# A two-layer hybrid decoder on one core: the second half of the first layer's down projection with the activations stationary, seven of its 22 steps by seven block products, its result turned in the next layer

## The reference, cut to what matters

```python
h = rms_norm(x, ffn_norm_w[l])
ff = (jax.nn.silu(h @ w_gate[l]) * (h @ w_up[l])) @ w_down[l]   # w_down: 5632 x 2048
x = x + ff
# next layer
h = rms_norm(x, attn_norm_w[l + 1])
proj = h @ w_in[l + 1]
```

## Time and profile before

| | us |
|---|---|
| median of 3 runs | 2095.04 |
| the three runs | 2094.85 to 2095.5 |
| profiled execution, whole | 2095.22 |
| its span, first to last instruction | 2093.5 |
| TensorE busy in the span | 2085.8 |
| DVE busy / ACT busy / POOL busy | 1408.1 / 1037.2 / 216.8 |

### The profile page before, as it was taken

One profiled execution on the slowest core, in us unless ns is written; L12 is line 12 of the kernel. 1 busy time (PEld: TensorE's weight loads), 2 busy tenths in 40 slices (PEclk: granted clock), 3 DMA queues, 4 the chain that ended last, 5 costly groups with the idle time before them and its releaser, 6 DMA issues.

```text
span 2093.5 us, 37778 instructions
## 1 busy us (share of the span) xinstructions
PE 2085.8 (100%) x16266; PEld 1965.1 (94%) x16266; DVE 1408.1 (67%) x1635; ACT 1037.2 (50%) x1289; POOL 216.8 (10%) x289
## 2 busy tenths in 40 slices
PE   9999999999999999999999999999999999999999
PEld 8987899999999999889999878999999999998887
DVE  7887866555555556876578878664555555558888
ACT  5555754444444444544445557454444444445454
POOL 1034200001000010000000432000110001100000
PEclk9999999999999999999999999999999999999999
DMA  7675366677767777776656644666777776778785
GB/s 229 187 213 150 127 201 191 192 203 205 215 203 203 206 205 223 248 227 191 193 171 192 202 141 150 193 189 183 202 203 213 207 203 202 205 221 259 240 264 188
DMA packets 213591, 420.81 MB, mean 201 GB/s; under 512 B 13408, under 2 KB 13808, under 8 KB 213424
## 3 DMA queue, kind: packets, MB, share of 16 engines
q1 hardware_dynamic: 202752, 390.24, 61.9%
q0 software_dynamic: 10640, 28.15, 4.5%
q10 hardware_dynamic: 32, 0.01, 0.0%
HBM read 406.78 MB, written 11.57 MB: 200 GB/s over the span
## 4 chain that ended last, share of the span: by engine, by line
PE 98%; ACT 1%; DMA 0%; DVE 0%; issue 0%; SPq 0%; ACTq 0%; DVEq 0%
PE ps L871 67%; PE ps L626 11%; PE ps L649 10%; PE ps L666 2%; PE ps L665 2%; PE ps L664 2%; PE ps L708 1%; PE ps L850 1%; DMA raw<-in_w_in_dram 0%; PE ps L828 0%; PE ps L827 0%; PE ps L803 0%; PE ps L788 0%; ACT w_hi_s L1065 0%; PE ps L750 0%
## 5 line engine op out<-in xcount | busy, mean ns | idle before, releaser
L1354 DVE TENSOR_TENSOR w_lo_s<-raw,w_hi_s 128x1024 fp32r<-128x1024 f32 x504 | 624.9, 1241 | 528.0 <-ACT w_hi_s L1065 526.8
L871 PE MATMUL ps<-h_hi,w_hi_s 128*128 128x256 f32 x3192 | 883.7, 277 | 0.8 <-DVE xr L1446 0.8
L871 PE MATMUL ps<-h_hi,w_lo_s 128*128 128x256 f32 x3192 | 881.9, 276 | 0.0
L871 PE MATMUL ps<-h_lo,w_hi_s 128*128 128x256 f32 x3192 | 881.8, 276 | 0.0
L1065 ACT CAST w_hi_s<-raw 128x1024 fp32r<-128x1024 f32 x503 | 528.0, 1050 | 697.2 <-PE ps L871 675.4
L871 PEld LDWEIGHTS ps<-h_hi,w_hi_s 128*128 128x128 f32 x3192 | 599.4, 188 | 1.2 <-DVE xr L1446 1.0
L871 PEld LDWEIGHTS ps<-h_hi,w_lo_s 128*128 128x128 f32 x3192 | 599.5, 188 | 0.0
L871 PEld LDWEIGHTS ps<-h_lo,w_hi_s 128*128 128x128 f32 x3192 | 599.5, 188 | 0.0
L1065 ACT CAST w_hi<-raw 128x1024 fp32r<-128x1024 f32 x185 | 193.4, 1051 | 154.1 <-PE ps L649 64.2
L1354 DVE TENSOR_TENSOR w_lo<-raw,w_hi 128x1024 fp32r<-128x1024 f32 x185 | 230.1, 1256 | 44.0 <-ACT w_hi L1065 43.3
L871 PE MATMUL ps<-f_hi,w_hi_s 128*128 128x256 f32 x832 | 231.2, 278 | 0.4 <-DVE stage L1391 0.4
(11 more groups left out here) (272 smaller groups left out, 2260.7 us busy)
## 6 DMA issues: line engine op xcount, KB each, us to landing
...
```

The source lines that it names most:

```text
L871: done = nc.tensor.matmul(ps[:, bank + m // 2, m % 2 * TOK:(m % 2 + 1) * TOK], w[:, slot, k, m * P:(m + 1) * P], h[:, rows + k, :], start= ...
L1354: v_.tensor_tensor(lo[:, slot, :, :], raw[:, slot, :, :], hi[:, slot, :, :].bitcast(F32), ALU.subtract).then_inc(lo_split, 1)
```

## The change

Chunks 2 and 3 of layer 0 become a second run in the activations-stationary form (run 1; layer 1's runs are now 2 and 3), on the banks that layer 1's second run uses. Its steps 7, 9, ..., 19 are made by seven block products; steps 0 to 6 and the even ones are plain. The weights-stationary form and its buffers begin only with layer 1's pair 0, and `reaches_next` moves there. The result of the run is written to `t_raw` by `half_out(1, e)`, after the last two pairs of the layer. TensorE turns it in layer 1, chunk 2 after pair 0 and chunk 3 after pair 1. Chunks 0 and 1 are turned after step 1 of run 1. Layer 1's pair 0 now waits for `half_out(1, 0)`. In layer 1 DVE and ACT add, split and square chunks 2 and 3 in steps 0 to 6, and what hangs on the norm moves: `x_total` from after pair 5 to after pair 8, `dt_products` and `spread_rs` from 8 to 10, `channels` from 9 to 11, `conv` from 9-12 to 11-14, `silu` from 13 to 15. `conv_out` stays after pair 16. The running sums of squares move from `stage` to `vtok`.

```diff
     DOWN = FT // 2
-    STEPS = range(3, 20, 2)
+    STEPS = [range(3, 20, 2), range(7, 20, 2), range(3, 20, 2), range(3, 20, 2)]
...
 
     def weights_stationary(pair):
         layer, p = pair // PAIRS, pair % PAIRS
-        return p < 4 * PPG or P_OUT <= p < P_DOWN or p >= P_LATE and layer < DEPTH - 1
+        return p < 4 * PPG or P_OUT <= p < P_DOWN
...
+        if p < P_DOWN:
             return None
         half, rest = divmod(p - P_DOWN, 2 * DOWN)
-        return layer + half, rest // 2, rest % 2
+        return 2 * layer + half, rest // 2, rest % 2
 
     def seven(pair):
 
         step = down_step(pair)
-        return step is not None and step[1] in STEPS
+        return step is not None and step[1] in STEPS[step[0]]
 
     def seven_before(run, q):
 
-        return run * len(STEPS) + len([s for s in STEPS if s < q])
...
 
-        return 2 * ((layer * GROUPS_ALL + idx) % 2)
+        return 2 * (idx % 2)
 
     def in_bank(layer, g):
...
-        square_sums, chunk_sums = stage[:, 1, 0, 0:TOK], stage[:, 1, 0, TOK:2 * TOK]
+        kept_sums = vtok[:, :, :, :].rearrange("p t j d -> p (t j d)")
+        square_sums, chunk_sums = kept_sums[:, 0:TOK], kept_sums[:, TOK:2 * TOK]
 
         class Steps:
...
+            def turn_half(n):
+
+                pe.wait_ge(half_kept, n + 1)
+                turned(4 + 2 * (n % 2), chunk_tiles(lambda t: t_raw[:, t, n % 2, :]), half_turned)
...
                     elif layer:
-                        pe.wait_ge(down_added, layer * DCH - 1 + g)
+                        pe.wait_ge(half_kept, 4 * layer - 1 + g)
...
-                        if layer and p == 5:
+                        if layer and p in (0, 1):
+                            turn_half(2 + p)
+                        if layer and p == 8:
                             x_total(layer, 0)
...
-                        if p == 8:
+                        if p == (10 if layer else 8):
...
-                    if layer:
+                for run in range(2 * layer, 2 * layer + 2):
+                    if run == 2:
                         pe.wait_ge(back_ready, DCH)
-                    else:
+                    elif run == 0:
                         pe.wait_ge(vec_ready, layer + 2)
                     for q in range(DOWN):
-                        pair = base + P_DOWN + ((run - layer) * DOWN + q) * 2
-                        if run < DEPTH and q % 2 == 0:
+                        pair = base + P_DOWN + ((run - 2 * layer) * DOWN + q) * 2
+                        if run % 2 == 0 and q % 2 == 0:
                             pe.wait_ge(ff_lo, layer * FCH + (q // 2 + 1))
-                        if run < DEPTH and q == STEPS[0]:
+                        if run % 2 == 0 and q == STEPS[run][0]:
                             pe.wait_ge(gate_scaled, layer * FCH + FCH)
                             pe.wait_ge(ff_ready, layer * FCH + FCH)
-                        if run == DEPTH and q == 0:
+                        if run % 2 and q == 0:
                             pe.wait_ge(sums_added, run)
-                        if run == DEPTH and q == STEPS[0]:
+                        if run % 2 and q == STEPS[run][0]:
                             pe.wait_ge(down_added, layer * DCH + 2)
                         if seven(pair):
                             seven_products(pair, run, q)
...
-                    pe.wait_ge(sums_added, layer + 1)
-                    for q in range(DOWN):
-                        pair = base + P_DOWN + n * DOWN + q
-                        products_turned(pair % RING, pair, 2 * q, down_bank(layer, n), q == 0, q == DOWN - 1, f_hi, f_lo)
-                        if n == 2 and q == 4:
-                            for e in range(2):
-                                pe.wait_ge(half_kept, e + 1)
-                                turned(4 + 2 * e, chunk_tiles(lambda t: t_raw[:, t, e, :]), half_turned)
+                        if run == 1 and q == 1:
+                            for n in range(2):
+                                turn_half(n)
+
 
 
         @block.scalar
...
-                reaches_next = P_OUT <= p < P_OUT + RING - 1 or weights_stationary(pair) and P_LATE <= p < P_LATE + RING - 1
+                reaches_next = P_OUT <= p < P_OUT + RING - 1 or pair >= PAIRS and p < RING - 1
                 act.wait_ge(pair_used, pair + (2 if reaches_next else 1))
                 if not seven(pair) or down_step(pair)[2] == 0:
...
                         x_square((0, 1, 4, 5).index(p))
-                    if layer and p == 1:
-                        x_hi(layer, 0, 3)
-                        x_chunk_squares(layer, 0, 3)
-                    if p == 8:
+                    if layer and p in (2, 4):
+                        act.wait_ge(half_turned, 4)
+                        x_hi(layer, 0, 1 + p // 2)
+                    if layer and p in (3, 5):
+                        x_chunk_squares(layer, 0, p // 2 + 1)
+                    if p == (10 if layer else 8):
                         rsb_out(layer, 0)
                     if p % 8 == 7 and 32 < p < 63:
                         evacuate(layer, p // 8)
...
                         nc.scalar.activation(dte[:, :], togo[:, :], ACT.Exp).then_inc(ecum_ready, 1)
-                    if 13 <= p < 38 and p % 8 == 5:
+                    if p == (15 if layer else 13) or 21 <= p < 38 and p % 8 == 5:
...
                         keep_first(down_step(base + p)[0])
-                    if layer + 1 < DEPTH and p >= P_LATE:
-                        n, q = (p - P_DOWN) // DOWN, (p - P_DOWN) % DOWN
-                        if n == 2 and q in (8, 12):
-                            x_hi(layer + 1, 0, q // 4 - 2)
-                        if n == 2 and q in (9, 13):
-                            x_chunk_squares(layer + 1, 0, q // 4 - 2)
-                        if n == 3 and q == 1:
-                            x_hi(layer + 1, 0, 2)
-                        if n == 3 and q == 2:
-                            x_chunk_squares(layer + 1, 0, 2)
+                    if down_step(base + p) in ((1, 4, 0), (1, 5, 0)):
+                        n = down_step(base + p)[1] - 4
+                        act.wait_ge(down_added, n + 1)
+                        x_chunk_squares(layer + 1, 0, n)
+                    if down_step(base + p) in ((1, DOWN - 2, 1), (1, DOWN - 1, 0)):
+                        x_hi(layer + 1, 0, down_step(base + p)[1] - DOWN + 2)
 
 
...
 
-            def half_out(e):
-
-                dve.wait_ge(pair_used, P_LATE - 1 + e + RING)
+            def half_out(run, e):
+
+                dve.wait_ge(pair_used, P_DOWN + 2 * (run + 1) * DOWN - 1 + e + RING)
                 for t in range(T):
                     added = stage[:, (0, 1, 0, 1)[2 * t + e], (0, 0, 1, 1)[2 * t + e], :]
-                    last = v_.tensor_tensor(t_raw[:, t, e, :], ps[:, four_banks(0)[t][e], :], added, ALU.add)
+                    last = v_.tensor_tensor(t_raw[:, t, e, :], ps[:, four_banks(run)[t][e], :], added, ALU.add)
...
 
-                if n < 2:
-                    dve.wait_ge(half_turned, n + 1)
-                else:
-                    dve.wait_ge(pair_used, layer * PAIRS + (P_DOWN + (n + 1) * DOWN + RING))
+                dve.wait_ge(half_turned, n + 1)
                 v = xr[:, :, n * N:(n + 1) * N]
...
                         split_lo(ahead_pair)
-                    if layer and p == 1:
-                        x_lo(layer, 0, 3)
-                    if layer and p == 3:
-                        sum_squares(layer, 0, 3)
-                    if p == 6:
+                    if layer and p in (0, 2, 4):
+                        x_lo(layer, 0, 1 + p // 2)
+                    if layer and p in (1, 3):
+                        add_down(layer - 1, 2 + p // 2)
+                    if layer and p in (5, 6):
+                        sum_squares(layer, 0, p - 3)
+                    if p == (9 if layer else 6):
                         if layer:
                             x_sum(layer, 0)
                         else:
                             first_sum()
+                    if p == (8 if layer else 6):
                         weigh_dt(layer)
                     if layer == 0 and p in (2, 3, 6, 7):
                         keep_x((2, 3, 6, 7).index(p))
-                    if p == 9:
+                    if p == (11 if layer else 9):
                         dt_out(layer)
                     if p == 13:
                         dt_in(layer)
                     if p == 15:
                         softplus(layer)
-                    if p == 9 or 15 <= p < 32 and p % 8 == 7:
-                        channels(layer, p // 8 - 1 if p == 9 else p // 8)
-                    if 9 <= p < 37 and p % 8 in (1, 2, 3, 4):
+                    if p == (11 if layer else 9) or 15 <= p < 32 and p % 8 == 7:
+                        channels(layer, p // 8 if p % 8 == 7 else 0)
+                    if p in ((11, 12, 13, 14) if layer else (9, 10, 11, 12)):
```

(24 more changed lines are left out.)

36 lines of the change are left out of this document (14 added, 22 removed).

## The result

| | median us | lowest to highest | runs |
|---|---|---|---|
| before | 2094.97 | 2094.50 to 2095.89 | 17 |
| after | 2099.34 | 2098.70 to 2100.12 | 17 |

The ratio is 1.002, with a 95% interval from 1.0013 to 1.0027. The kernel became slower by 4.4 us, 0.21%, 0.2 us over the 4.2 us that the prediction set as the bound for "can be told from no change"; the interval has that bound in its middle. The time lies inside the range, but 1.7 us above the likeliest value. The profiled execution of after took 2100.09 us (span 2098.4; before 2095.22 and 2093.5).

What follows compares the result with a forecast made beforehand. TensorE's work was taken to bound the kernel. Terms -6.0 + 1.8 + 0.5 + 4.5 + 0.6 + 0.9 + 0.2 = +2.5 us took the median from 2095.04 to 2097.6, range 2095.0 to 2100.8.

Steps and rivals of the forecast that it cites:

- TensorE's work exchanged: End of run 0 to layer 1's first product: 122.96 us give way to 116.97, a gain of 6.0 us.
- pause at the seam: Before layer 1's pair 0: TensorE waits 4.5 us for half_out(1, 0) behind DVE's queue.
- turning, slower pace, restarts: Layer 1: 16 added transposes 1.8 us, slower products after breaks 0.5, restarts after the three waits 0.2.
- wait at `x_total`: Layer 1 after pair 8: TensorE waits some 0.6 us for DVE's last sum of squares.
- wait at `conv_out`: Layer 1 after pair 16: TensorE waits 0.9 us for silu, behind the conv pieces and dt_in.
- clock: TensorE's clock after the seam's pause: the main sum has it stay at its level, costing nothing.
- rival A: Clock falls at the seam, adding 1.4 to 3 us: 2099.0 to 2100.6; chance 0.27.
- Rivals B: Only the seam's wait comes, the two later ones in layer 1 are hidden: 2096.0 us; chance 0.15.
- rival C: Seam waits no longer than before, DVE reaching half_out before pair 2's low part: 2092 us; chance 0.06.
- The side: Whole kernel: slower (above 2099.2 us) 0.25, the same 0.72, faster (below 2090.8) 0.03.

Runs made afterwards that it cites:

- run 1: Not a follow-up: the stretch of the kernel after in which chunks 2 and 3 of layer 0 are made in the activations-stationary form; 22 steps, seven of seven products.
- run 0: Not a follow-up: layer 0's first stretch in the activations-stationary form, in the kernels before and after, ahead of chunks 2 and 3; ends at 931.59 us in after.
- the one-step kernel: The seam kernel with a single seven-product step (19) in place of seven, in layer 0's second stretch; 2097.31 us.
- the seam kernel: Kernel after, with x_hi and x_lo of chunks 0 and 1 earlier, last sums_out and both half_out ahead of low parts of pairs 1 and 2; 2093.10 us.

## Why the prediction was right, and what it missed

| term | computed | measured |
|---|---|---|
| TensorE's work exchanged | -6.0 | -6.13 |
| pause at the seam | +4.5 | +4.61 |
| turning, slower pace, restarts | 1.8 + 0.5 + 0.2 = +2.5 | +2.43 (what the others leave) |
| wait at `x_total` | +0.6 | +0.65 |
| wait at `conv_out` | +0.9 | +0.82 |
| clock | 0 (rival A: 1.4 to 3) | +2.02 |
| sum | +2.5 | +4.40 |

- **The stretch exchanged.** Right to 0.13 us: 0.2 were set aside for the seam between the runs, and it costs nothing there. Rows of the same kernel, a plain and a seven-product step of run 0, told run 1 exactly, and the one-step kernel showed that the seven-product steps lose nothing.
- **The seam.** Right to 0.1 us, with the very rows that were named: TensorE pauses for `sums_out`, `x_lo`, the low part of pair 2 and half of `half_out`. It was got by writing down DVE's queue from T = 0 with durations from the earlier trace rows. Moving `half_out` ahead of one row shortened the pause by that row's 1.14, and putting the seam right took all but 0.55 of it; moved ahead of two rows it was no longer what ended the wait, and `x_lo` was. Rivals B and C didn't occur; the seam kernel, 1.1 us above what rival C gave, shows what C would have been with the two later waits still there.
- **Turning and pace.** The sum came out, but one premise of it is too wide. "After each break the weights-stationary form runs slower" holds behind some breaks only: behind the transposes of 1103.93 the trace of before goes on at 113 to 114 ns a product, and pair 0 of the kernel with the seam put right was at 113 ns after six products. That the 0.5 was about right is in part luck.
- **The later waits.** Both right within 0.1 us, although each is a difference of two sums of about 17 us. That one of them can be moved away for good and the other not wasn't in the prediction.
- **The clock.** This is the step that failed. The forecast took the clock as staying at its level, since no wait in the trace of before was long enough to speak, and left the fall to rival A with a chance of 0.27. The fall happened, and cost 2.02 in the profile, inside rival A's 1.4 to 3, though over the 1.4 to 1.7 that were worked out for it: 2097.6 + 2.0 = 2099.6 stands against 2099.34 measured. What spoke for it in the rows was the slow start, which shows the lower level after TensorE had done nothing; against it stood a wait of 1 us (the longest in mid-run is 0.8), which bears on no pause of 4.5. Of the two the slow start was the nearer row, and the case should have been the likeliest. The Trainium skill ("TensorE: Matmul & The Clock Gate", Part 1) has idleness throttle TensorE to 1.2 GHz and sustained work release it; the trace agrees, with 213 ns a product for 20 products behind the pause, 114 to 118 after them, and no slow product when the pause was filled.
- **The side.** The time lies in the range because the range had been drawn to take in rival A, not because the sum was complete. With the clock the result lies at the bound of 0.2% itself: 0.21%, with an interval from 0.13% to 0.27%. "The same" at 0.72 was too sure; with the chances for rival A the other way round the two sides would have been about even.

Open: why the number of slow products differs from kernel to kernel and run to run. The profiles have 14 to 20 of them in kernels with the same pause of 4.6 us, which is 1.4 to 2.0 us, and the 17 runs of after spread over 1.4. That these belong together is likely, but only the profiled executions can be counted. Where between 1.9 and 2.7 us of pause the clock begins to fall, and whether it is the same length each time, is open too.
